# Feed-forward stage of a decoder layer: order of the SyncE loads, who copies the first product, and who makes the last first sum

## What is computed

```
D_MODEL = 1024
D_FF = 4 * D_MODEL
...
    x = x + o @ w_o
    h = jnp.square(jax.nn.relu(rms_norm(x, g_f) @ w1))
    return x + h @ w2
```

## Time and profile before

| what | value |
|---|---|
| three runs | 2779.66, 2781.75, 2782.03 us |
| profiled execution: its time, its span | 2772.16 us, 2770.4 us |
| TensorE busy (matmul) over the span | 90% |
| VectorE, ScalarE, GpSimd busy | 52%, 31%, 17% |
| mean granted TensorE clock | 0.945 of full |
| `stage_ffn` in the profile | about 2039 to 2753 us |

### The profile page before, as it was taken

How to read it: one execution, slowest core, us unless ns; L and a number is a source line. 1 busy time by engine, 2 the same in 40 slices (tenths; PEclk the granted TensorE clock), 3 DMA queues, 4 the chain that set the end, 5 groups by cost and what they waited for, 6 DMA issues and landing times. The chain is left out here.

```text
span 2770.4 us, 51404 instructions
## 1 busy us (share of the span) xinstructions
PE 2494.1 (90%) x21934; PEld 2246.8 (81%) x21934; DVE 1435.6 (52%) x2393; ACT 852.1 (31%) x1420; POOL 474.0 (17%) x408
## 2 busy tenths in 40 slices
PE   5998799978997789996999999998879999899998
PEld 5996698946995455555999999996669999899998
DVE  4445666443335677734122324343387766865675
ACT  4324322221124344453121212114332222432332
POOL 1001333203001233410000000000023223332331
PEclk8997799978997899998999999999889999999999
DMA  8320100045221111256111113204014464642432
GB/s 290 112 77 23 18 4 4 4 156 87 79 63 38 69 61 46 92 195 221 46 47 48 49 49 87 76 8 167 1 63 167 134 219 137 216 162 94 155 130 80
DMA packets 182308, 261.46 MB, mean 94 GB/s; under 512 B 19270, under 2 KB 147697, under 8 KB 172760
## 3 DMA queue, kind: packets, MB, share of 16 engines
q1 hardware_dynamic: 171267, 194.18, 22.4%
q0 software_dynamic: 9888, 61.87, 6.3%
q10 hardware_dynamic: 926, 2.12, 0.2%
HBM read 199.88 MB, written 62.61 MB: 95 GB/s over the span
## 5 line engine op out<-in xcount | busy, mean ns | idle before, releaser
L3634 PE MATMUL ps<-ff_operand_high,ff_weight_parts 128*128 128x264 f32 x1024 | 295.7, 289 | 21.5 <-DVE x L3849 7.1
L3636 PE MATMUL ps<-ff_operand_high,ff_weight_parts 128*128 128x264 f32 x1024 | 293.1, 286 | 0.0
L3635 PE MATMUL ps<-ff_operand_low,ff_weight_parts 128*128 128x264 f32 x1024 | 292.8, 286 | 0.0
L3634 PE MATMUL ps<-ff_sums_high,ff_weight_parts 128*128 128x264 f32 x768 | 222.3, 289 | 22.5 <-DVE ff_weight_parts L3765 20.5
L3636 PE MATMUL ps<-ff_sums_high,ff_weight_parts 128*128 128x264 f32 x768 | 221.1, 288 | 0.0
L3635 PE MATMUL ps<-ff_sums_low,ff_weight_parts 128*128 128x264 f32 x768 | 220.8, 287 | 0.0
L3634 PEld LDWEIGHTS ps<-ff_operand_high,ff_weight_parts 128*128 128x128 f32 x1024 | 194.7, 190 | 25.7 <-issue 14.2
L3636 PEld LDWEIGHTS ps<-ff_operand_high,ff_weight_parts 128*128 128x128 f32 x1024 | 195.0, 190 | 0.0
L3635 PEld LDWEIGHTS ps<-ff_operand_low,ff_weight_parts 128*128 128x128 f32 x1024 | 194.9, 190 | 0.0
L3086 PE MATMUL ps<-xn_h,me_gate_w_high 128*128 128x352 f32 x576 | 187.2, 325 | 5.3 <-DVE me_gate_w_low L3152 5.3
L3087 PE MATMUL ps<-xn_l,me_gate_w_high 128*128 128x352 f32 x576 | 185.9, 323 | 0.0
(11 more groups left out here) (739 smaller groups left out, 6875.9 us busy)
## 6 DMA issues: line engine op xcount, KB each, us to landing
ff_raw<-in_w_ff SPq DMA_DIRECT2D x64, 512.0 KB, 5.9
ff_staged<-hidden_operands SPq DMA_DIRECT2D x22, 1056.0 KB, 5.0
hidden_operands<-ff_hidden SPq DMA_DIRECT2D x16, 1056.0 KB, 4.3
hidden_operands<-ff_hidden_sums SPq DMA_DIRECT2D x16, 792.0 KB, 7.0
me_gate_w_raw<-in_w_in SPq DMA_DIRECT2D x23, 512.0 KB, 3.9
pj_raw<-in_w_in SPq DMA_DIRECT2D x13, 512.0 KB, 4.6
ff_x_staged<-hidden_operands SPq DMA_DIRECT2D x6, 1056.0 KB, 12.7
xn_high<-xn_h POOLq DMA_DIRECT2D x1, 4224.0 KB, 14.3
```

The lines of the kernel that those rows point to most:

```text
L3634: e.matmul(o[:, cols], wring[:, r, 0, k, :], high(i)[:, k, cols], start=first, stop=False, skip_group_check=True)
L3635: e.matmul(o[:, cols], wring[:, r, 0, k, :], low(i)[:, k, cols], start=False, stop=False, skip_group_check=True)
L3636: mm = e.matmul(o[:, cols], wring[:, r, 1, k, :], high(i)[:, k, cols], start=False, stop=k == 3, skip_group_check=True)
```

## The change

Four edits, all in `stage_ffn`:

1. SyncE: `half(2u+3)` goes ahead of `store(u-1)`.
2. SyncE: the two operand sets at the end of u = 19 and 23 (14, 15 and 21, 22) go behind `half(2u+3)` of the next unit (`half(43)`, `half(51)`).
3. P1 of the units 16 to 19 is copied into `g1[m]` by ScalarE, ahead of its `weights_high(q+3)`; TensorE's P2 of these units waits for that copy (`s_g1`), and VectorE has a wait for it and a drain in place of its copy.
4. The difference for P7 at the entry is made by VectorE behind `weights_low(2)`, not by GpSimd; the semaphore `s_T1`, for which only GpSimd waited, goes.

```
@@ SyncE
             for u in range(NU):
+                g, m = divmod(u - NPAIR, 4)
+                if 2 * u + 3 < 2 * NU:
+                    half(2 * u + 3)
                 if 1 <= u < NPAIR:
                     store(u - 1)
-                if 2 * u + 3 < 2 * NU:
-                    half(2 * u + 3)
+                if u > NPAIR and m == 0:
+                    for n in range(7 * (g + 1), 7 * (g + 1) + 2):
+                        if n < 28:
+                            stage(n)
...
-                g, m = divmod(u - NPAIR, 4)
...
-                if u >= NPAIR and m == 3 and g < 2:
-                    for n in range(7 * (g + 2), 7 * (g + 2) + 2):
-                        stage(n)
@@ GpSimd
-            e.wait_ge(s_T1, 1)
-            e.wait_ge(s_T4, 1)
-            e.tensor_tensor(whole(P7)[:, :, :], whole(P3)[:, :, :], whole(P7)[:, :, :], ALU.subtract).then_inc(s_T3, 1)
@@ TensorE, room
-                if i == P2:
+                if i == P2 and v < 4:
+                    e.wait_ge(s_g1, v + 1)
+                elif i == P2:
                     e.wait_ge(s_td, 7 * v + P1 + 1)
@@ ScalarE
+                if NPAIR <= u < NPAIR + 4 and i == P1:
+                    e.wait_ge(s_mm, q + 1)
+                    if u == NPAIR:
+                        e.wait_ge(s_tv, 5 * (u - 1) + 4)
+                    if u == NPAIR + 2:
+                        e.wait_ge(s_sb, 16 * NPAIR)
+                    e.activation(g1[u - NPAIR], bank(u, 0), ACT.Copy).then_inc(s_g1, 1)
@@ VectorE, take_down and entry
-                        if m == 2:
-                            e.wait_ge(s_sb, 16 * NPAIR)
-                        mm = e.tensor_copy(g1[m], bank(u, 0))
+                        e.wait_ge(s_g1, m + 1)
+                        mm = e.drain()
...
-            e.drain().then_inc(s_T1, 1)
+            e.drain()
...
             weights_low(2)
+            first_sum(P7, P3, P7, 2)
+            e.drain().then_inc(s_T3, 1)
```

More of the change, by code:

```diff
@@ L3517, in stage_ffn @@
         s_var, s_root, s_n = (K.sem("ff_end_" + n) for n in ("mean", "root", "normed"))
-        s_T1, s_T2, s_T3, s_T4, s_hA, s_z = (K.sem("ff_" + n) for n in ("t1_set", "t2_set", "t3_set", "t4_set", "high_set", "first_ready"))
+        s_T2, s_T3, s_T4, s_hA, s_z = (K.sem("ff_" + n) for n in ("t2_set", "t3_set", "t4_set", "high_set", "first_ready"))
+        s_g1 = K.sem("ff_first_product_kept")
         s_xd, s_xs, s_xr = K.sem("ff_x_kept"), K.sems("ff_x_staged", 4), K.sems("ff_x_back", 4)
```

## The result

The changed kernel takes 2759.7 us (median of 5 runs, 2753.45 to 2763.42), the kernel before in its own 5 runs 2779.66 us. The ratio is 0.9934, 95% interval 0.9913 to 0.9954: faster by 0.66%.

A forecast was written before the change was run, and what follows sets the result against it. TensorE, at 90% of the span, was taken as the bound, so only its idle or 1.2 GHz time could return. 6.6 + 5.15 + 2.2 + 2.1 - 0.15 = 15.9 us off 2781.75 gave 2765.9 us, range 2761 to 2774.

The forecast's parts named there:

- Edit 2, 6.6 and 5.15 us: Units 20/21 and 24/25: windows would hold about 156 matmuls, as at unit 28, giving back 6.6 and 5.15 us.
- Rival A: Units 20 and 24: TensorE still stops 2 us or more, earlier up-unit loads give nothing; 2774.0 us, chance 0.15.
- Edit 1, 2.2 us with 3.3 as upper bound: Up units: weights loaded ahead of the store land 3 to 4.5 us earlier; 2.2 us back, bounds 0 and 3.3.
- 1.9 us idle plus about 0.25 us of restart at each of some seven stops: Up units: TensorE's idle time and restarts bound what earlier weight loads can give, upper bound 3.3 us.
- Edit 3 and unit 16, 2.1 us: Unit 16: VectorE loses the P1 copy and some holding by GpSimd's sums; 2.1 us back, bounds 0.6 and 3.2.
- the 0.6: Unit 16: gain if only the P1 copy leaves VectorE, 0.71 us less an estimated 0.1 for the drain.
- one operation is then still held, 1.1 us, so about 1.4 us comes back: Unit 16: GpSimd's sums, about 5 us earlier, hold VectorE 1.1 us instead of an estimated 2.5; about 1.4 us back.
- Edit 4, 0.15 us worse, at most 2.4: Entry: P6 starts 4.4 us sooner, but P7 waits for VectorE's taking of P6; 0.15 us worse, bounds 0.3 better, 2.4 worse.
- B: Entry: the 4.4 us gain is kept since P7 waits less for VectorE; 20.5 us faster, 2761.3 us, chance 0.08.
- C: Up units: earlier GpSimd sums hold VectorE and TensorE waits, 2.2 us lost per unit; 17 us slower, 2799 us, chance 0.04.
- D: Up units: load and store share the engines, so reordering them gives nothing; 12.3 us faster, 2769.5 us, chance 0.18.
- E: Rival A with the worst entry (2.4 us) and no gain at unit 16; 4.0 us faster, 2777.8 us, chance 0.05.

The follow-up runs named there:

- the lists reordered: Kernel after, at the entry P1 copied and P6 taken early, P7 taken ahead of P3's low part, GpSimd's unit 1 sums behind that part; ratio to before 0.9933.
- the held kernel: Kernel after, but GpSimd begins the sums of unit 1 only when the sixth low operand part (P4's) is set; ratio to before 0.9944.
- P6 taken early: Kernel after, but at the entry ScalarE copies P1 before waiting for the last first sum and VectorE takes P6 right behind it; ratio to before 0.9935.

## Why the prediction was nearly right, and where it was wrong

- *Edit 2, 6.6 and 5.15 us:* right in mechanism and size, 6.67 and 5.24, alone 6.44 and 5.27. The model was a place in the same trace, unit 28, with the same work and no obstacle; it foretold even the 1.1 us wait that stayed, and the 156 matmuls of each window (157 and 156). Rival A is refuted.
- *Edit 1, 2.2 us with 3.3 as upper bound:* 3.75, above the bound. The step that failed is "1.9 us idle plus about 0.25 us of restart at each of some seven stops": all of the 1.92 us idle went, and 1.83 us more, where I allowed 1.75 as a ceiling and took far less as likely. The bound of 3.3 was also added up wrongly: its own two terms give 3.67.
- *Edit 3 and unit 16, 2.1 us:* mis-sized, -1.05. P2's gate and P7's wait of about 3 us came as written. The copy gave 0.46 us in unit 16 for the 0.6, and 0.43 went again in unit 19, costed at nothing: the 1.05 are edit 1's. There the failed step is "one operation is then still held, 1.1 us, so about 1.4 us comes back". In before GpSimd's sums of unit 16 held two operations by 1.1 us each (2392.27 and 2393.97); moved 6.3 us earlier against P1 of unit 15 they hold three, 2.5 us in all, and P3 of unit 15 now waits 0.87 us. So no holding went away. What did come is an earlier VectorE (its taking of P6 lies 2.3 us earlier against P1). First the rows of before, then those of after:
```profile
2392.27 1.77 DVE L3765 TENSOR_TENSOR ff_weight_parts<-ff_raw,ff_weight_parts 128x512 fp32r<-128x512 f32 x1
2393.97 3.44 DVE L3776 TENSOR_TENSOR ff_operand_low<-ff_x_staged,ff_operand_high 128x2112 fp32r<-128x2112 f32 x1
...
2412.42 1.18 DVE L3765 TENSOR_TENSOR ff_weight_parts<-ff_raw,ff_weight_parts 128x512 fp32r<-128x512 f32 x1
2413.52 3.45 DVE L3776 TENSOR_TENSOR ff_sums_low<-ff_x_staged,ff_sums_high 128x2112 fp32r<-128x2112 f32 x1
```
```profile
2386.43 1.79 DVE L3773 TENSOR_TENSOR ff_weight_parts<-ff_raw,ff_weight_parts 128x512 fp32r<-128x512 f32 x1
...
2388.77 1.17 DVE L3773 TENSOR_TENSOR ff_weight_parts<-ff_weights_s,ff_weight_parts 128x512 fp32r<-128x512 f32 x1
2389.99 3.31 DVE L3784 TENSOR_TENSOR ff_sums_low<-ff_x_staged,ff_sums_high 128x2112 fp32r<-128x2112 f32 x1
...
2413.26 3.45 DVE L3784 TENSOR_TENSOR ff_sums_low<-ff_x_staged,ff_sums_high 128x2112 fp32r<-128x2112 f32 x1
```
  The forecast also overlooked GpSimd's sums of unit 17. They hold VectorE in unit 16 in before as in after (3.45 us at 2413.52 and at 2413.26), so they are no loss of the change; but held back they returned 2.6 us more.
- *Edit 4, 0.15 us worse, at most 2.4:* the step that failed. The starts up to P7 came as forecast: P6 4.49 us sooner (4.4), P2 behind ScalarE's copy, the taking of P6 and P7 itself within 0.1 us of before. One reason did not: P7 does not wait for that taking (before 0.57 us, in after 0.03), because P2 at 1.2 GHz ends just behind it. The sum stopped at P7. The sums of unit 1 stood in my text nowhere: in before they had waited for VectorE's low parts of P4's weights and of P3's operand, now they held both, 2.2 us, P4 waited for that, and the 1.2 GHz behind made 3.6 of it. Begun 0.9 us later they cost nothing. That they go first in this kernel and not in before is shown; by what rule is not.
- *The total:* -15.9 forecast, -13.07 in the stage: 3.5 us of loss missed at the entry, 1.05 of gain too much in units 15 to 19, 1.55 too little in the up units. That the median still came out below the forecast is luck: the stage gained 13.07 us, 0.47% of the kernel, and the two medians differ by 19.96 (the interval of the ratio spans 12.8 to 24.2 us). The rest is in no row of the stage; it is of the size of the scatter between runs. The execution of before that was profiled was 9.6 us under the median of the first three runs, the one of after on its median, and the stage's first matmul moves by over 11 us between profiles.
- *Rivals:* B's gain exists only with the lists reordered, and then 2.5 us of 4.4. C is refuted, D too. E, which needs A, falls with it. The four single edits add up to -12.4 us against -13.07 together.

## What to carry to other kernels

Moving an issue that blocks the queue out from ahead of a load brought more than anything else here: where the same trace has a place without the obstacle, its rows gave the gain within 0.1 us. When work moves between VectorE and GpSimd, follow both lists on past the product where the gain is given back, up to the next operation of either that reads SBUF. A stall of TensorE of 2.5 us was followed here by a stretch at 1.2 GHz, so 2.2 us of held operations became 3.7 us.

## What the runs showed of the hardware

- Which of the two engines goes first is not settled by whose instruction starts first. In the held kernel GpSimd's sum starts at 2078.44, VectorE's next low part at 2078.82, and VectorE's takes its plain 2.35 us while GpSimd stands; before, a sum begun at 2074.81 let two such operations pass (4.22 us). With P6 taken early, a sum begun at 2078.89 held the low part begun at 2079.14 (3.44 us). The Trainium skill ("SBUF — State Buffer", section "Who interferes with whom") says that the order of issue decides who blocks. By the starts in these traces it holds in the last case and not in the first two; whether the start of a row is the moment of issue no run shows. Nor was it GpSimd's earlier work or the moment of the load (experiments above). How long ScalarE's high part had been there sorts the cases at P4's weights, untested.
- Where GpSimd's sum went first at the entry it cost the next VectorE operation 1.1 us, a 128x2112 one (3.44 instead of 2.35) as well as a 128x512 one (1.78 instead of 0.68). Where the sum had already run under a taking, which reads PSUM and one SBUF tile, the low part behind it lost 0.5 us (1.16 in the held kernel, 1.17 at 2388.77 in after).
- The stretch at 1.2 GHz in unit 16 lies at different products in otherwise equal kernels. In after P7 begins at full clock (0.36 us) and P4 waits 2.50 us; in the kernel with edit 4 undone P7 begins with a matmul of 0.56 us, P4 does not wait, and P3 comes 0.6 us sooner relative to P6. The cause is open.
